# Gated rows of five FFNs turned in 32x32 blocks by VectorE, the blocks moved by DMA copies on SyncE's queue, in place of TensorE's transposes

## The reference

```
def swiglu(h, w1, w3, w2):
    return (jax.nn.silu(h @ w1) * (h @ w3)) @ w2

def swiglu_2(h, w_in, w_out):
    gate, up = jnp.split(h @ w_in, 2, axis=-1)
    return (jax.nn.silu(gate) * up) @ w_out
```

## Time and profile before

| | |
|---|---|
| median of three executions | 1701.77 us |
| span of the profiled execution | 1700.2 us |
| TensorE busy (matmul) | 1674.0 us, 98% of the span, 8120 matmuls |
| VectorE busy | 1095.2 us, 64%, 1265 instructions |
| ScalarE busy | 823.4 us, 48%, 1022 instructions |
| DMA queue of SyncE (q1) | 236016 packets, 321.95 MB, 57.0% of 16 engines |
| packets under 512 bytes, all queues | 11040 of 240129 |
| clock granted to TensorE | full in nearly every slice |

### The profile page before, as it was taken

One profiled execution on the slowest core, in us unless ns is written; L12 is line 12 of the kernel. 1 busy time (PEld: TensorE's weight loads), 2 busy tenths in 40 slices (PEclk: granted clock), 3 DMA queues, 4 the chain that ended last, 5 costly groups with the idle time before them and its releaser, 6 DMA issues.

```text
span 1700.2 us, 20774 instructions
## 1 busy us (share of the span) xinstructions
PE 1674.0 (98%) x8120; PEld 1354.4 (80%) x8120; DVE 1095.2 (64%) x1265; ACT 823.4 (48%) x1022; POOL 48.2 (3%) x60
## 2 busy tenths in 40 slices
PE   6999999999999999999999999999999999999999
PEld 3775888887678888788888888888888888888887
DVE  3898688896867654755468865554655458865552
ACT  3427654436464443644447564443544357554441
POOL 0001000000000000000003000000000003000000
PEclk9999999999999999999999999999999999999999
DMA  9695289895547655755554346545665554346550
GB/s 352 232 308 178 83 293 307 314 354 197 195 130 257 223 210 173 216 182 190 186 176 159 100 122 209 191 181 166 201 194 187 185 173 149 100 140 207 185 187 25
DMA packets 240129, 332.29 MB, mean 195 GB/s; under 512 B 11040, under 2 KB 192004, under 8 KB 240032
## 3 DMA queue, kind: packets, MB, share of 16 engines
q1 hardware_dynamic: 236016, 321.95, 57.0%
q10 hardware_dynamic: 2704, 5.82, 1.0%
q0 software_dynamic: 1312, 3.19, 0.7%
HBM read 329.87 MB, written 1.05 MB: 195 GB/s over the span
## 4 chain that ended last, share of the span: by engine, by line
PE 89%; DVE 6%; ACT 2%; issue 1%; DMA 1%; SPq 0%; DVEq 0%
PE bank L458 19%; PE bank L460 19%; PE bank L459 18%; PE bank L828 7%; PE bank L833 7%; PE bank L829 7%; PE bank L954 2%; DVE lo L1941 1%; PE bank L1151 1%; PE bank L1338 1%; PE bank L1339 1%; PE bank L1341 1%; PE bank L808 1%; DMA raw<-in_ada_w 1%; ACT hi L1394 1%
## 5 line engine op out<-in xcount | busy, mean ns | idle before, releaser
L1941 DVE TENSOR_TENSOR lo<-raw,hi 128x2048 fp32r<-128x2048 f32 x246 | 564.0, 2296 | 339.6 <-ACT hi L1394 339.2
L1394 ACT ACTIVATE hi<-raw 128x2048 fp32r<-128x2048 f32 x258 | 492.3, 1912 | 317.2 <-PE bank L460 172.2
L458 PE MATMUL bank<-hi,XTh 128*128 128x512 f32 (+1 forms) x1424 | 564.1, 396 | 4.9 <-DVE XTl L2052 4.5
L460 PE MATMUL bank<-hi,XTl 128*128 128x512 f32 (+1 forms) x1424 | 552.6, 388 | 0.0
L459 PE MATMUL bank<-lo,XTh 128*128 128x512 f32 (+1 forms) x1424 | 551.9, 388 | 0.0
L458 PEld LDWEIGHTS bank<-hi,XTh 128*128 128x128 f32 x1424 | 267.9, 188 | 67.6 <-issue 14.0
L460 PEld LDWEIGHTS bank<-hi,XTl 128*128 128x128 f32 x1424 | 267.8, 188 | 56.1
L459 PEld LDWEIGHTS bank<-lo,XTh 128*128 128x128 f32 x1424 | 268.2, 188 | 52.5 <-issue 1.0
L828 PE MATMUL bank<-hi,HTh 128*128 128x512 f32 x528 | 206.9, 392 | 0.0
L829 PE MATMUL bank<-lo,HTh 128*128 128x512 f32 x528 | 205.5, 389 | 0.0
L833 PE MATMUL bank<-hi,HTl 128*128 128x512 f32 x528 | 163.6, 389 | 0.0
(11 more groups left out here) (386 smaller groups left out, 1420.0 us busy)
## 6 DMA issues: line engine op xcount, KB each, us to landing
raw<-in_ffn_w_in SPq DMA_DIRECT2D x176, 512.0 KB, 4.8
raw<-in_ffn_w SPq DMA_DIRECT2D x132, 512.0 KB, 4.8
raw<-in_ada_w SPq DMA_DIRECT2D x96, 512.0 KB, 5.3
raw<-in_ffn_w_out SPq DMA_DIRECT2D x88, 512.0 KB, 3.8
raw<-in_w_mix_in SPq DMA_DIRECT2D x52, 512.0 KB, 4.7
raw<-in_od_pw_w SPq DMA_DIRECT2D x24, 512.0 KB, 5.8
raw<-in_ev_w_in SPq DMA_DIRECT2D x20, 512.0 KB, 9.6
raw<-in_w_mix_out SPq DMA_DIRECT2D x16, 512.0 KB, 4.1
```

The lines of the kernel that those rows point to most:

```text
L458: pe.matmul(dst, xh, wh, start=start, stop=False)
L460: return pe.matmul(dst, xl, wh, start=False, stop=stop)
L1394: act.activation(hi[r][:, :], raw[g % RAW][:, :], ACT.Copy).then_inc(*up("hi", d))
L1941: dve.tensor_tensor(lo[r][:, :], raw[g % RAW][:, :], hi[r][:, :].bitcast(F32), ALU.subtract).then_inc(*up("lo", d))
```

## The change

Five FFNs (`MOVED`, p = 2, 3, 5, 6, 8; not p = 0) no longer use TensorE's transposes. In their place:

- VectorE turns each 32 x 32 block of `HID` within itself and writes the chunk into a new tile `BLK` (`block_turn`, right after the chunk's two products, one instruction of 128 x 512).
- SyncE's queue carries the blocks to their places across the partitions, from `BLK` to a new tile `HTR` (`move_blocks`): for each pair (a, b) of four partition groups, one DMA takes from source group a the columns of block b, 32 numbers (128 bytes) at a time, to destination group b, columns of block a. That is 16 DMAs for a batch; the batches are chunks 0 to 2, 3 to 5, 6 to 8, and 9 to 10. A batch stands in the queue ahead of the slab whose buffer is freed by the split behind the batch's last chunk.
- ScalarE and VectorE write `HTh` and `HTl` from `HTR` in SBUF, at other places in their order (`SPLIT_UP` gives them by chunk of the up projection, `SPLIT_DOWN` by slab of the down projection).
- TensorE waits ahead of each down slab for the parts of that chunk, and the first down slab has the usual order. ScalarE waits for the product of the chunk before, ahead of `SG`; VectorE waits for its own block turn ahead of `HID`.

`BLK` lies on `HTh`'s bytes and `HTR` on `HTl`'s.

```
--- before.py
+++ after.py
@@ -266,6 +266,13 @@
 FFN_GATE = {0: (0, 5), 2: (1, 5)}
 FFNS = {0: 0, 2: 1, 3: 2, 5: 3, 6: 4, 8: 5}
 MIXES = {4: 0, 7: 1}
+BATCHES = ((0, 1, 2), (3, 4, 5), (6, 7, 8), (9, 10))
+MOVED = (2, 3, 5, 6, 8)
+SPLIT_UP = {5: (0, 1), 6: (2,), 8: (3, 4), 9: (5,), 10: (6,)}
+SPLIT_DOWN = {0: (7,), 1: (8,), 4: (9, 10)}
 GAINS = {3: "ffn1_0", 4: "mix2_0", 5: "ffn2_0", 6: "ffn1_1", 7: "mix2_1", 8: "ffn2_1"}
@@ -312,6 +319,8 @@
         ht_at = used_bytes[0]
         HTh = place("HTh", [P, KF, S], F32R)
         HTl = place("HTl", [P, KF, S], F32R)
+        BLK = tile_at("BLK", [P, KF, S], ht_at)
+        HTR = tile_at("HTR", [P, KF, S], ht_at + 4 * KF * S)
         gate_at = used_bytes[0]
         GATE = place("GATE", [P, 2, D])
         used_bytes[0] = gate_at + 14592
@@ -966,14 +975,15 @@
                         half_turn(l, mod, h, bank[7])
                 if normed_first(p):
-                    first_chunks(p, lambda: turn_chunk(0, bank[4]), lambda: None)
+                    first_chunks(p, (lambda: None) if p in MOVED else (lambda: turn_chunk(0, bank[4])), lambda: None)
                 else:
                     first_chunk(p)
                 for c in range(2 if normed_first(p) else 1, NC):
                     if c >= 2:
                         pe.wait_ge(*at("hidden", (f, c - 2, 1)))
                     half_chunk(d + 2 * c, 0, x_groups(c))
-                    turn_chunk(c - 1, bank[4])
+                    if p not in MOVED:
+                        turn_chunk(c - 1, bank[4])
                     if p in SHIFTED:
                         ada_sums(c)
                     half_chunk(d + 2 * c + 1, 1, x_groups(c))
@@ -985,8 +995,9 @@
                     turn_chunk(NC - 1, bank[2])
                 def last_hidden(s):
-                    if s == NC - 1:
-                        pe.wait_ge(*at("ht_lo", (f, NC - 1)))
+                    if p in MOVED or s == NC - 1:
+                        pe.wait_ge(*at("ht_hi", (f, s)))
+                        pe.wait_ge(*at("ht_lo", (f, s)))
                 def ada_in_down(s):
@@ -997,8 +1008,11 @@
                     pe.wait_ge(*at("gate_full", (*FFN_GATE[p], 1)))
                 if p == 0:
                     pe.wait_ge(*at("mods", (1, 1, 0, "full")))
-                down(p + 1, HTh, HTl, late, before=last_hidden, after=ada_in_down if p == 0 else None,
-                     head=turn_bank_free)
+                if p in MOVED:
+                    down(p + 1, HTh, HTl, None, before=last_hidden)
+                else:
+                    down(p + 1, HTh, HTl, late, before=last_hidden, after=ada_in_down if p == 0 else None,
+                         head=turn_bank_free)
             def before_w_out(s):
@@ -1672,6 +1686,12 @@
                     act.activation(HTh[:, 2 * c:2 * c + 2, :], b[:, :].rearrange("p (k s) -> p k s", k=2),
                                    ACT.Copy).then_inc(*up("ht_hi", (f, c)))
+                def moved_high(c):
+                    n = next(i for i, batch in enumerate(BATCHES) if c in batch)
+                    act.wait_ge(*at("ht_moved", (f, n, 3, 3)))
+                    act.activation(HTh[:, 2 * c:2 * c + 2, :], HTR[:, 2 * c:2 * c + 2, :], ACT.Copy).then_inc(*up("ht_hi", (f, c)))
                 for c in range(NC):
                     if c == 0:
                         first_chunk(p)
@@ -1686,9 +1706,14 @@
                             bias_rows(1, 5)
                     else:
                         split(d + 2 * c + RING)
-                        turn_chunk(c - 1, bank[4])
+                        if p not in MOVED:
+                            turn_chunk(c - 1, bank[4])
+                        for n in SPLIT_UP.get(c, ()) if p in MOVED else ():
+                            moved_high(n)
                     act.wait_ge(*at("used", d + 2 * c + 1))
                     for t in range(T):
+                        if c and p in MOVED:
+                            act.wait_ge(*at("hidden", (f, c - 1, t)))
                         act.activation(SG[:, t, :], bank[2 * (c % 2) + t][:, 0:HALF], ACT.Silu,
                                        scale=1.0 if p in SHIFTED else ST[:, t:t + 1]).then_inc(*up("gated_ffn", (f, c, t)))
                     split(d + 2 * c + 1 + RING)
@@ -1698,7 +1723,14 @@
                 def late():
                     turn_chunk(NC - 1, bank[2])
-                down(p + 1, late)
+                def moved_in_down(s):
+                    for n in SPLIT_DOWN.get(s, ()):
+                        moved_high(n)
+                if p in MOVED:
+                    down(p + 1, None, moved_in_down)
+                else:
+                    down(p + 1, late)
             down(0, None)
             ffn(0)
@@ -2428,6 +2460,16 @@
                     src = b[:, :].rearrange("p (k s) -> p k s", k=2)
                     low("ht_lo", (f, c), HTl[:, 2 * c:2 * c + 2, :], src, HTh[:, 2 * c:2 * c + 2, :], at("ht_hi", (f, c)))
+                def moved_low(c):
+                    ks = slice(2 * c, 2 * c + 2)
+                    low("ht_lo", (f, c), HTl[:, ks, :], HTR[:, ks, :], HTh[:, ks, :], at("ht_hi", (f, c)))
+                def block_turn(c):
+                    dve.wait_ge(*at("hidden", (f, c, 1)))
+                    dve.transpose(BLK[:, 2 * c:2 * c + 2, :].rearrange("p k (t n) -> p k t n", t=T),
+                                  HID[:, :, :].rearrange("p t (k n) -> p k t n", k=2)).then_inc(*up("ht_blocks", (f, c)))
                 def ffn_mods(c):
                     gates, shifts = halves_of(FFN_ADA[p][c - 2])
                     for l, mod, h in gates:
@@ -2442,18 +2484,25 @@
                             dve.wait_ge(*at("rstd2", p))
                     else:
                         split(d + 2 * c + RING)
-                        turn_chunk(c - 1, bank[4])
+                        if p not in MOVED:
+                            turn_chunk(c - 1, bank[4])
+                        for n in SPLIT_UP.get(c, ()) if p in MOVED else ():
+                            moved_low(n)
                         if p in SHIFTED and c >= 2:
                             ffn_mods(c)
                     for t in range(T):
                         b = bank[2 * (c % 2) + t]
                         dve.wait_ge(*at("gated_ffn", (f, c, t)))
+                        if c and p in MOVED:
+                            dve.wait_ge(*at("ht_blocks", (f, c - 1)))
                         if p in SHIFTED:
                             last = dve.tensor_tensor(HID[:, t, :], SG[:, t, :], b[:, HALF:CH], ALU.mult)
                         else:
                             last = dve.scalar_tensor_tensor(out=HID[:, t, :], in0=b[:, HALF:CH], scalar=ST[:, t:t + 1],
                                                             in1=SG[:, t, :], op0=ALU.mult, op1=ALU.mult)
                         last.then_inc(*up("hidden", (f, c, t)))
+                    if p in MOVED:
+                        block_turn(c)
                     split(d + 2 * c + 1 + RING)
                     if p in SHIFTED:
                         for unit in FFN_ADA[p][c]:
@@ -2469,7 +2518,14 @@
                         half_mods(l, mod, h, bank[1])
                     for unit in DOWN_ADA[s]:
                         ada_quarter(*unit)
-                down(p + 1, late, ada_in_down if p == 0 else None)
+                def moved_in_down(s):
+                    for n in SPLIT_DOWN.get(s, ()):
+                        moved_low(n)
+                if p in MOVED:
+                    down(p + 1, None, moved_in_down)
+                else:
+                    down(p + 1, late, ada_in_down if p == 0 else None)
             down(0, None)
             ffn(0)
@@ -2926,8 +2982,26 @@
                                            ALU.subtract).then_inc(*up("hg_tail", l))
         def sync_engine(sp):
-            for g, (_, parts) in enumerate(slabs):
+            def move_blocks(p, n):
+                f, batch = FFNS[p], BATCHES[n]
+                if n:
+                    sp.wait_ge(*at("ht_moved", (f, n - 1, 3, 3)))
+                sp.wait_ge(*at("ht_blocks", (f, batch[-1])))
+                ks = slice(2 * batch[0], 2 * batch[-1] + 2)
+                for a in range(4):
+                    for b in range(4):
+                        src = BLK[32 * a:32 * a + 32, ks, :].rearrange("i k (t n) -> i (k t) n", t=T)
+                        dst = HTR[32 * b:32 * b + 32, ks, :].rearrange("i k (t n) -> i (k t) n", t=T)
+                        sp.dma_start(dst[:, :, 32 * a:32 * a + 32], src[:, :, 32 * b:32 * b + 32]).then_inc(
+                            *up("ht_moved", (f, n, a, b), 16))
+            moves = {first[f"up{p}"] + 2 * batch[-1] + 1 + RING + RAW: (p, n)
+                     for p in MOVED for n, batch in enumerate(BATCHES)}
+            for g, (index, parts) in enumerate(slabs):
                 r = g % RAW
+                if index in moves:
+                    move_blocks(*moves.pop(index))
                 if g >= RAW:
```

(2 more changed lines are left out.)

40 lines of the change are left out of this document (35 added, 5 removed).

## The result

The changed kernel took 1676.28 us (median of four executions, 1674.97 to 1677.77) against 1701.96 us for the kernel before in the same session: a ratio of 0.9847, with a 95% interval of 0.9833 to 0.9860, or 25.7 us less. The forecast was 1675.8. The profiled execution took 1675.14 us with a span of 1673.8; that span is 26.4 us shorter than the one of before.

A forecast was written before the change was run, and what follows sets the result against it. TensorE, busy 98% of the span, was taken to set the FFNs' pace. Removing 55 groups gives -26 us with nothing returned: span 1674.2, plus 1.6 to the median, 1675.8 us; own range 1674 to 1680, overall range 1673 to 1697.

The forecast's parts named there:

- TensorE's price of a group: Five FFNs: each of 55 groups of four transposes removed saves 0.47 us of TensorE's time, 26 us in all.
- TensorE's new waits: Ahead of each down slab, waits for the chunk's high and low parts, and the first slab's changed order: nothing.
- ScalarE: High-part copies from SBUF: 0.63 us against 0.58 from PSUM, hidden by its 2.86 us wait for TensorE in each chunk.
- VectorE's block turn: Between product and split in each chunk: 0.69 us, bounds 0.48 and 2.30, free within a 1.39 us wait for ScalarE.
- The copies: SyncE's queue: 320 DMAs, a batch holds the queue 8 to 9 us, with nothing on the path.
- Issue: SyncE's queue: 16 DMAs a batch at 0.45 us each, 7.2 us during which the next slab is not issued.
- Engine time: DMA engines: 14.5 ns of one engine per piece, 384 pieces per engine and batch, 5.6 us, taken as 6.
- How fast pieces are made: Copies' pieces: 2.7 ns each for all engines together, so a batch is made in at most 16.8 us.
- The cover: Weight slabs ahead of ScalarE's splits: 19 us to spare, 13 in the FFN behind the convolution; an 8 to 9 us batch fits.
- Rival 1: Copies' pieces come slowly, 10.7 ns each, and weights wait behind them: about 2330 us, deciding from about 4 ns; chance 0.19.
- Rival 2: Batches take 20 to 30 us, TensorE stops 2 to 4 us in each FFN: 1683 to 1696 us; chance 0.09.
- Rival 3: Gaps at TensorE's transpose groups only hide other waits that come back: no change, 1699 to 1704 us; chance 0.03.

The follow-up runs named there:

- e2: Changed kernel with TensorE's 220 transposes put back beside the new route, their results unused in the five FFNs: 1702.62 us.
- e6: Changed kernel with only FFN p = 5 moved, the other FFNs left as before: 1697.08 us, 0.9968 of the kernel before.
- e7: Changed kernel with VectorE doing each block turn three times, same values written again: 1676.42 us.
- e8: Changed kernel with two batches of copies per FFN (chunks 0 to 5, 6 to 10) in place of four, 160 DMAs: 1676.25 us.
- e3: Changed kernel with each block copy cut in two by row tile, 640 DMAs with the same pieces: 1691.27 us.
- e5: Changed kernel with the sixth FFN (p = 0) moved too, copies in four batches on SyncE's queue: 1696.07 us.
- e12: Changed kernel with all six FFNs moved, four batches of copies issued by GpSimd, later halves written one step later: 1675.35 us.
- e10: Changed kernel with all six FFNs moved and the copies issued by GpSimd in four batches: 1679.42 us.

## Why the prediction was right

**TensorE's price of a group: right.** 55 x 0.47 = 26 us; measured 25.7 in the median, 26.4 in the span and 26.2 in TensorE's busy time. The interval of the median (23.8 to 28.4) holds both the 26 by the period and the 24.7 by the gap; the distance of one FFN tells them apart, 5.21 us against 5.17 by the period and 4.95 by the gap. e2 gives the term back in full and e6 shows it for one FFN.

**TensorE's new waits nothing: right.** The waits are those of before, and the down projection starts at the same distance.

**ScalarE: right.** The copy from SBUF took 0.61 us where I had 0.63, and there is no new wait of TensorE.

**VectorE's block turn: right.** 0.711 us against the 0.69 taken, within bounds of 0.48 and 2.3. Of the 1.39 us of wait, 0.74 was used (0.71 and the start of the next instruction). e7 shows that even three times the turn is covered. The Trainium skill (VectorE: DVE Perf Modes, The TRN2 errata) gives (N + 151) / 0.96 ns for a float32 addition of two tensors, 691 ns for 512 elements. The differences of 128x512 here agree (0.68 to 0.69), and the block turn, for which the section gives nothing, lies 3% above.

**The copies: nothing on the path, right; three sizes off.**
- Issue: I took 0.45 us from the issues of weight loads. Measured 0.62 in the median and 0.66 with all between, so 16 are 10.5 us and not 7.2. The batches take 10.4 to 12.4 us, not 8 to 9.
- Engine time: I took 14.5 ns a piece from the earlier trace rows; measured 13.7 in one batch, and over the program (0.630 x 1673.8 - 0.570 x 1700.2) x 16 / 117760 = 11.6 ns. The Trainium skill (DMA: Bandwidth & Descriptors, Why small descriptors are slow) says that such a transfer escapes the small-piece penalty and led to an estimate of 8.2 ns. The measured ones are 1.4 to 1.7 times that. The time did not hang on it. In the up projection the DMA share went from 0.59 to 0.75, in the down projection from 0.50 to 0.54, below the 77 to 80% that I worked out for the first.
- How fast pieces are made, which I could bound only by 16.8 us a batch: this never showed. 5871 packets passed in 10.7 us with the engines half idle, 1.8 ns each, and twice the pieces per DMA cost 0.02 us more to issue (e8).

**The cover: enough, but by less than the sum said.** In p = 2 I counted 13 us for the queue and 8 to 9 for a batch, which leaves 4 to 5. The batch took 11.1, and some 2 were left. The issue term was too small by nearly a third, and it was luck that the tightest place had room for the difference: the sum had not asked for it. Behind it I counted another 12 us on TensorE's side. e3 bears that out in size: the late slab alone would have stopped TensorE for 3.0 us. What the count leaves out is that work in ScalarE's order behind the late split is late as well, which made it 5.0. I had named that path for batch 2 alone ("ScalarE's silu and its splits would queue behind"). I also took each batch by itself, while e3 shows that a long hold is carried over to the next. I priced a batch of 17 us in p = 2 as unseen by TensorE. No run has a batch of 17 there, so where the loss begins between 12.4 and 22.6 us stays open.

**Rival 1, slower (0.19): fell.** It decides from 4 ns a piece. The row on which it rested, 10.7 ns from one packet to the next with the engines 8.5% busy, did not carry over: pieces came at 1.8 ns. The Trainium skill (VectorE: DVE Perf Modes, The three transpose paths) warns that a plain copy which transposes by strides is 19 times slower than the transposing DMA. Nothing like it showed here, where each piece is 128 contiguous bytes; no run has a copy by strides or the transposing DMA, so the factor itself was not measured.

**Rival 2, half given back (0.09): not this kernel, but a neighbour.** Its condition, batches of 20 to 30 us, is met by e3 at 22.6 us, and its 1683 to 1696 holds e3's 1691.27. Half of its account came true: ScalarE waited for copies, up to 13.5 us in chunk 10, and the thin cover of the first changed FFN was used up. But TensorE did not stop 2 to 4 us in each FFN: 7.1 us of waits fell in p = 2 and 1.0 in the others, and the clock behind the stops cost 5.2 more.

**Rival 3, no change (0.03): fell.** No wait took the place of the groups.

## What to carry to other kernels

Where one engine is busy 98% of the time and the chain is on it, what leaves its queue is gained in full as long as nothing else becomes late; e5 and e12 show where that ends. The price of a small group is best read as the difference between two periods of the pattern, with and without it. Many small copies on the queue that also brings the weights are priced first by issues times the time of one issue, here 0.66 us for 8 to 24 pieces per partition, and not by bytes: compare one batch with the slack between the issue and the use of the load behind it, at the tightest place, and make the DMAs fewer or give them another queue before that slack is used up. Cover on the other engines is worth less where work that needs no weights stands in an engine's order behind work that does.

## What the runs showed of the hardware that I had not expected

- A copy within SBUF of 32 partitions takes 0.62 us to issue with up to 12 pieces of 128 bytes per partition and 0.64 with up to 24, on SyncE's queue (medians); on GpSimd's it takes 0.62 too, and lands in 3.9 instead of 2.0 us.
- A stop of TensorE of a few microseconds cost more than its length here, since a stretch at the lower clock level followed: in e3 8.1 us of new waits came with 5.2 us by the clock, in e5 18.3 (with 1.3 for `MODS`) with 10.2, in e10 5.2 with 3.6 (0.91 in each of two stretches of 20 us). Behind e3's stop of 2.1 us the clock from 660 to 680 us was 0.91; behind e12's new waits, at most 1.8 us at a time, it was 1.00.
- The mean clock of a whole execution is too coarse for such a sum: between 20 and 40 us, ahead of any copy, e3 has 0.83 and the changed kernel 0.91, which is 1.6 us of the difference, and e10 has 0.91 between 460 and 480 us, another 1.8 us, where it has no new wait. Read the clock by stretches behind the stop.
- Float32 block turns of 128x512 took 710 to 714 ns, all 55 of them, whatever else ran.
